# Expert turns with the two down pieces in third and fourth place, a TensorE sum of expert rows, and later stores of normed rows

## The reference, cut to what matters

```python
    def expert_block(args):
        xblk, e = args
        gate, up = jnp.split(xblk @ w13[e], 2, axis=-1)
        return (jax.nn.silu(gate) * up) @ w2[e]
    contrib = yb[dest] * sw[:, None].astype(h.dtype)
    return jax.ops.segment_sum(contrib, stok, num_segments=T)
    f = _hier_moe(u2, w_route_g, b_route_g, w_route_e, b_route_e, w_moe_13, w_moe_2)
    x = _layernorm(ALPHA * x + (1 + g2) * f, ln_ffn_g, ln_ffn_b)
```

## Time and profile before

| what | value |
|---|---|
| median of 3 runs | 2646.61 us (2645.77 to 2648.37) |
| the profiled execution | 2651.25 us, its span 2649.5 us |
| PE busy in the span | 2383.2 us (90%) |
| DVE, ACT, POOL busy | 1628.0, 1164.9, 543.3 us |
| mean granted TensorE clock | 0.956 |

### The profile page before, as it was taken

One profiled execution on the slowest core, in us unless ns is written; L12 is line 12 of the kernel. 1 busy time (PEld: TensorE's weight loads), 2 busy tenths in 40 slices (PEclk: granted clock), 3 DMA queues, 4 the chain that ended last, 5 costly groups with the idle time before them and its releaser, 6 DMA issues. The chain is left out here.

```text
span 2649.5 us, 32426 instructions
## 1 busy us (share of the span) xinstructions
PE 2383.2 (90%) x13016; PEld 1987.3 (75%) x13016; DVE 1628.0 (61%) x2532; ACT 1164.9 (44%) x1453; POOL 543.3 (21%) x309
## 2 busy tenths in 40 slices
PE   4999899999999999999999999999389999999960
PEld 2978888898888887667999978744267777777740
DVE  5269889889898870000333311176668888888869
ACT  2336766776766762000000000000167777777751
POOL 1211212212212120001443311000022332322320
PEclk8899999999999999999999999999599999999985
DMA  9272232233223215121111221211479999999953
GB/s 330 89 266 65 75 107 75 79 84 95 79 68 112 82 45 178 32 56 37 44 48 48 71 82 40 84 63 50 159 248 347 340 350 351 359 343 346 341 199 144
DMA packets 247177, 398.08 MB, mean 150 GB/s; under 512 B 17997, under 2 KB 168149, under 8 KB 243917
## 3 DMA queue, kind: packets, MB, share of 16 engines
q1 hardware_dynamic: 224050, 345.35, 39.3%
q0 software_dynamic: 14048, 34.39, 3.4%
q10 hardware_dynamic: 8928, 16.26, 1.9%
HBM read 365.23 MB, written 48.14 MB: 156 GB/s over the span
## 5 line engine op out<-in xcount | busy, mean ns | idle before, releaser
L2002 PE MATMUL bank<-u_hi,w_pairs 128*128 128x344 f32 x1344 | 450.4, 335 | 1.4 <-DVE u_lo L1353 1.4
L2004 PE MATMUL bank<-u_hi,w_pairs 128*128 128x344 f32 x1344 | 434.6, 323 | 0.0
L2003 PE MATMUL bank<-u_lo,w_pairs 128*128 128x344 f32 x1344 | 434.3, 323 | 0.0
L1737 DVE TENSOR_TENSOR we_parts<-u_whole,we_parts 128x2048 fp32r<-128x2048 f32 x129 | 295.1, 2288 | 57.9 <-ACT we_parts L1178 57.7
L1178 ACT ACTIVATE we_parts<-u_whole 128x2048 fp32r<-128x2048 f32 x129 | 247.1, 1917 | 51.4 <-PE bank L2283 26.5
L794 POOL TENSOR_TENSOR w_pairs<-arena,w_pairs 128x1024 fp32r<-128x1024 f32 x56 | 151.7, 2710 | 564.7 <-ACT w_pairs L954 564.5
L2002 PEld LDWEIGHTS bank<-u_hi,w_pairs 128*128 128x128 f32 x1344 | 257.7, 192 | 12.2 <-issue 10.5
L2003 PEld LDWEIGHTS bank<-u_lo,w_pairs 128*128 128x128 f32 x1344 | 257.3, 191 | 3.8 <-issue 3.8
L2004 PEld LDWEIGHTS bank<-u_hi,w_pairs 128*128 128x128 f32 x1344 | 257.1, 191 | 0.0
L2141 PE MATMUL bank<-arena 128*128 128x344 f32 x768 | 222.2, 452 | 0.0
L2281 PE MATMUL bank<-we_parts,x_parts 128*128 128x512 f32 x512 | 209.7, 410 | 3.3 <-DVE we_parts L1737 1.8
(11 more groups left out here) (345 smaller groups left out, 4956.2 us busy)
## 6 DMA issues: line engine op xcount, KB each, us to landing
u_whole<-in_w_moe_dram SPq DMA_DIRECT2D x128, 1024.0 KB, 7.4
arena<-in_w_moe_dram SPq DMA_DIRECT2D x64, 1024.0 KB, 7.4
arena<-in_w_in_dram SPq DMA_DIRECT2D x88, 512.0 KB, 5.4
arena<-in_w_ada_dram SPq DMA_DIRECT2D x24, 1024.0 KB, 7.1
arena<-cum_dram ACTq DMA_DIRECT2D x62, 256.0 KB, 3.2
yb_dram<-arena POOLq DMA_DIRECT2D x8, 1032.0 KB, 5.2
arena<-in_state_ssm_dram SPq DMA_DIRECT2D x16, 512.0 KB, 5.1
out_dram<-arena SPq DMA_DIRECT2D x16, 512.0 KB, 5.1
```

Source lines behind the costliest of these rows:

```text
L1737: dve.tensor_tensor(w_los[v], wraw[slot], w_his[v].bitcast(F32), ALU.subtract).then_inc(wlo_ready, 1)
L2002: pe.matmul(out, hi[:, k, :], u_hi[:, k, at], start=(k == 0), stop=False)
L2003: pe.matmul(out, hi[:, k, :], u_lo[:, k, at], start=False, stop=False)
L2004: last = pe.matmul(out, lo[:, k, :], u_hi[:, k, at], start=False, stop=(k == KD - 1))
```

## The change

Three parts. **Start:** the four head loads go behind the first weight unit and count on another semaphore, which TensorE awaits before its first dt product; VectorE's copy of `dskb` goes behind the last tile's low part; GpSimd awaits all eight products of the first conditioning third before its first store of normed rows. **Expert turns:** the order of pieces becomes gate 0, gate 1, down 0, down 1, gate 2, gate 3, on SP, ScalarE, VectorE and TensorE; h is turned after the whole of gate 0; ScalarE's output copies go behind the split of the sixth piece, VectorE's first subtraction ahead of the low part of h. In the drain there are two dummy slices. **End:** VectorE makes 18 diagonal matrices of routing weights once (`spread_f`, 128 x 2304); TensorE multiplies them with `fa` and `fb` and sums in the accumulator, four matmuls of 512 columns a tile, two tiles in flight; VectorE multiplies the sum by the gate in two halves. ScalarE's scaling and VectorE's L1908 go.

```diff
-                     (dtb, ...), (alog, ...), (dskb, ...), (w_dt, ...)]
+                     (rows_s[5:29, :], t["state_ssm_conv"][0].rearrange("b r d -> (b r) d"))]
+            heads = [(dtb, ...), (alog, ...), (dskb, ...), (w_dt, ...)]
...
-            for u in range(6):
+            load_unit(0, group_cols(0)[0])
+            for dst, src in heads:
+                sp.dma_start(dst, src).then_inc(finw_landed, 16)
+            for u in range(1, 6):
                 load_unit(u, group_cols(0)[u])
...
             pool.wait_ge(consts_ready, 1)
+            pool.wait_ge(mod_done, 8)
             for i in range(TILES + 1):
                 pool.wait_ge(x0_ready, i + 1)
...
-                        if j in (1, 2):
-                            load_w2(j - 1, before)
+                        if j in (2, 3):
+                            load_w2(j - 2, before)
                         else:
-                            load_w13(j, max(j - 2, 0), expert)
+                            load_w13(j, j if j < 2 else j - 2, expert)
...
             def expert_turn(b, n, stored):
                 silu(1 - b, n - 1)
                 w_high(n, 2)
                 h_high(1 - b, n - 1)
                 w_high(n, 3)
                 w_high(n, 4)
-                out_rows(1 - b, n - 1, n * 6 + 1, stored)
                 w_high(n, 5)
+                out_rows(1 - b, n - 1, n * 6 + 2, stored)
...
             w_high(extra * 2 + (2 * PAIRS), 2)
             h_high(1, extra * 2 + (2 * PAIRS - 1))
+            w_high(extra * 2 + (2 * PAIRS), 3, True)
...
-                act.wait_ge(fin_landed[i % 3], 32 * (i // 3 + 1))
-                act.activation(fa[i % 3][0:rows, :], fa[i % 3][0:rows, :], ACT.Copy,
-                               scale=wts[0:rows, i:i + 1]).then_inc(f_scaled, 1)
...
             def expert_turn(b, n, column, done_column):
                 h_both(1 - b, n - 1)
+                w_low(n, 2)
                 h_low(1 - b, n - 1)
-                for j in range(2, 6):
+                for j in range(3, 6):
                     w_low(n, j)
...
+            dve.tensor_tensor(spread_f, widen(ident, 1, 2 * NI), widen(wts, 2, P), ALU.mult).then_inc(spread_f_ready, 1)
...
-                fin.did(dve.scalar_tensor_tensor(x, fb[i % 3][0:rows, :], wts[0:rows, NI + i:NI + i + 1], x,
-                                                 ALU.mult, ALU.add))
-                fin.settle()
-                fin.did(dve.tensor_tensor(x, x, g2, ALU.mult))
+                dve.wait_ge(f_summed, i + 1)
+                for half in range(2):
+                    at = slice(512 * half, 512 * half + 512)
+                    last = dve.tensor_tensor(x[:, at], banks[2 * (i % 2) + half][0:rows, :], g2[:, at], ALU.mult)
...
-                    gate_up(b, n, 0, 0, (0,))
+                    gate_up(b, n, 0, 0).then_inc(wparts_used, 1)
                     turn_h(1 - b, n - 1)
-                    gate_up(b, n, 0, 0, (1,)).then_inc(wparts_used, 1)
+                    gate_up(b, n, 1, 1).then_inc(wparts_used, 1)
...
-                    down(1 - b, n - 1, 0, 2, n * 6).then_inc(wparts_used, 1)
-                    down(1 - b, n - 1, 1, 0, n * 6 + 1).then_inc(wparts_used, 1)
+                    down(1 - b, n - 1, 0, 0, n * 6 + 1).then_inc(wparts_used, 1)
+                    down(1 - b, n - 1, 1, 1, n * 6 + 2).then_inc(wparts_used, 1)
-                gate_up(b, n, 1, 1 + skip).then_inc(wparts_used, 1)
                 turn_rows(1 - b, n + 1, 0, landed)
...
+            for i in range(TILES + 1):
+                rows = P if i < TILES else NS
+                pe.wait_ge(fin_landed[i % 3], 32 * (i // 3 + 1))
+                if i >= 2:
+                    pe.wait_ge(f_scaled, i - 1)
+                for half in range(2):
+                    for a, rows_of in enumerate((fa, fb)):
+                        last = pe.matmul(banks[2 * (i % 2) + half][0:rows, :], spread_f[0:rows, a * NI + i, 0:rows],
+                                         rows_of[i % 3][0:rows, 512 * half:512 * half + 512],
+                                         start=(a == 0), stop=(a == 1))
+                last.then_inc(f_summed, 1)
```

More of the change, by code:

```diff
@@ L696, in load_w2 @@
             def load_w2(x, expert):
-                sp.dma_start(wraw[1 + x].rearrange("p (k c) -> p k c", k=2),
-                             w2_v[:, ds(expert * 4 + 2 * x, 2), :]).then_inc(wraw_landed[1 + x], 16)
+                sp.dma_start(wraw[2 + x].rearrange("p (k c) -> p k c", k=2),
+                             w2_v[:, ds(expert * 4 + 2 * x, 2), :]).then_inc(wraw_landed[2 + x], 16)
             sp.wait_ge(wo_done, TILES + 1)
             sp.wait_ge(u2_ready, TILES + 1)
-            for x, j in enumerate((0, 3, 4, 5)):
+            for x, j in enumerate((0, 1, 4, 5)):
                 load_w13(j, x, 0)
@@ L732, in _ @@
             expert = expert_of(extra * 2 + (2 * PAIRS - 1))
-            sp.wait_ge(wlo_ready, extra * 12 + (12 * PAIRS - 7))
-            sp.dma_start(wraw[0][:, 0:P], w13_v[:, 0, 0:P]).then_inc(wraw_landed[0], 16)
             for x in range(2):
-                sp.wait_ge(wlo_ready, extra * 12 + (12 * PAIRS - 6 + x))
+                sp.wait_ge(wlo_ready, extra * 12 + (12 * PAIRS - 7 + x))
+                sp.dma_start(wraw[x][:, 0:P], w13_v[:, 0, 0:P]).then_inc(wraw_landed[x], 16)
+            for x in range(2):
+                sp.wait_ge(wlo_ready, extra * 12 + (12 * PAIRS - 5 + x))
                 load_w2(x, expert)
@@ L1149, in _ @@
                 rows = P if i < TILES else NS
-                act.wait_ge(mvar_ready, i + 1)
+                act.wait_ge(var_ready, TILES + 2 + i)
                 act.activation(mv2[0:rows, i % 2, 2:3], mv2[0:rows, i % 2, 1:2], ACT.Sqrt,
-                               bias=epsc[0:rows, :]).then_inc(mstd_ready, 1)
+                               bias=epsc[0:rows, :]).then_inc(std_ready, 1)
                 act.wait_ge(u2_turned, i + 1)
@@ L1167, in _, with w_high @@
             act.activation(wb, wb, ACT.Exp).then_inc(route_e, 1)
-            def w_high(n, j):
+            def w_high(n, j, last=False):
                 g = slot_no(n, j)
                 first = isinstance(n, int) and n == 0
-                slot = (0, 3, 4, 5)[j] if first else j
-                act.wait_ge(wraw_landed[slot], n * 16 + (0 if slot in (1, 2) else 16))
-                if not (first and j < 3):
+                slot = (0, 1, 4, 5)[j] if first else j
+                act.wait_ge(wraw_landed[slot], n * 16 + (0 if slot in (2, 3) else 16))
+                if last:
+                    act.wait_ge(wlo_ready, g - 2)
+                elif not (first and j < 3):
                     act.wait_ge(wparts_used, g - 2)
@@ L1293, in _ @@
             last.then_inc(cols_copied, 1)
-            dve.wait_ge(small_landed, 16 * 16)
-            for h in range(2):
-                st.did(dve.tensor_copy(dskip[HD * h:HD * h + HD, :],
-                                       dskb[HD * h:HD * h + HD, :].rearrange("p (j h) -> p h j", h=2)[:, h, :]))
             for half in range(2):
@@ L1311, in _ @@
                 norm(i)
+            dve.wait_ge(small_landed, 12 * 16)
             add_mod(0)
@@ L1360, in _ @@
             u_low(TILES)
+            dve.wait_ge(finw_landed, 64)
+            for h in range(2):
+                st.did(dve.tensor_copy(dskip[HD * h:HD * h + HD, :],
+                                       dskb[HD * h:HD * h + HD, :].rearrange("p (j h) -> p h j", h=2)[:, h, :]))
             dve.wait_ge(x0_stored, 9 * 16)
@@ L1732, in w_low @@
             def w_low(n, j):
-                slot = (0, 3, 4, 5)[j] if isinstance(n, int) and n == 0 else j
+                slot = (0, 1, 4, 5)[j] if isinstance(n, int) and n == 0 else j
                 v = parts_of(n, j)
@@ L1905, in _ @@
                 x = fa[i % 3][0:rows, :]
-                dve.wait_ge(fin_landed[i % 3], 32 * (i // 3 + 1))
-                dve.wait_ge(f_scaled, i + 1)
-                fin.did(dve.scalar_tensor_tensor(x, fb[i % 3][0:rows, :], wts[0:rows, NI + i:NI + i + 1], x,
-                                                 ALU.mult, ALU.add))
-                fin.settle()
-                fin.did(dve.tensor_tensor(x, x, g2, ALU.mult))
-                fin.settle()
+                dve.wait_ge(f_summed, i + 1)
+                if i == 0:
+                    fin.settle()
+                for half in range(2):
+                    at = slice(512 * half, 512 * half + 512)
+                    last = dve.tensor_tensor(x[:, at], banks[2 * (i % 2) + half][0:rows, :], g2[:, at], ALU.mult)
+                    if half == 0:
+                        fin.did(last)
+                last.then_inc(f_scaled, 1)
+                dve.wait_ge(f_scaled, i + 1)
                 fin.did(dve.scalar_tensor_tensor(x, x1[0:rows, i, :], ALPHA, x, ALU.mult, ALU.add))
```

44 lines of the change are left out of this document (26 added, 18 removed).

## The result

The kernel after takes 2589.92 us (median of 4 runs, 2588.68 to 2590.84), the kernel before 2647.49 (median of 4, 2645.77 to 2648.71): a ratio of 0.978, 95% interval 0.9769 to 0.9792, or 57.6 us less. The forecast was 2590 us. That the total is met to a tenth of a us is partly luck: the start gave 2 to 3 us less than forecast and the expert turn some 4 us more, as the table of marks shows. The profiled execution after took 2590.1 us (span 2588.3).

A forecast was written before the change was run, and what follows sets the result against it. Prediction: start waits for data, the expert turn is a 19.61 us chain of waits without transfers, VectorE bounds the end. Terms -6.7 - 45 + 0.5 - 5.7 = -56.9 us, from median 2646.61 to 2590 us; range 2580 to 2622.

The forecast's parts named there:

- Start, -6.7: Start: conditioning piece 3, and the third's addition with it, comes 6.7 us earlier; ends -3 and -7.2.
- the heads at 2.9: Start: the four head loads, some 1400 pieces of 128 bytes, leaving the queue give 2.9 us; ends 1.0 and 3.4.
- Expert turn, -45: Expert stage: the turn falls from 19.70 to 18.2 us, 30 intervals x 1.5, -45 us.
- the closed chain: Expert turn: longest chain of waits, from output copy through splits, subtractions, h and 36 matmuls to the second output copy, 18.2 us.
- the forecast's two bounds: Expert stage, weight rate: 358 GB/s gives 19.1 us a turn, -18 us; 412 GB/s gives no limit, -45 us.
- Drain, +0.5: After the last turn: first down piece waits for a subtraction instead of h's high part, +0.5 us; ends 0 and +2.3.
- End, -5.7: End: VectorE tiles -11.5 us, TensorE's first sum +4.3, later sums +1.5; together -5.7 us, ends -9 and -2.7.
- ring: End: later sums sit in three buffers, 6.0 to 7.2 us a tile; 7.0 taken for six tiles, +1.5 us.
- Weights as the bound: Rival, expert stage: at 358 GB/s the turn is 19.1 us, total -29.9, 2617 us; 27%.
- A new wait in the old one's place: Rival, expert turn: stays at 19.7 us, only start, drain and end count, -11.9, 2635 us; 8%.
- The scatter: Slower rival, expert turn: output copies wait for scatter landing; at 18 us landing the turn is 20.9, 2671 us; 6%.
- The ends at nothing: Rival: sums stay at half clock, stores collide with weight units; both ends give nothing, the turn its 45, 2602 us; 6%.

The follow-up runs named there:

- The exchange on ScalarE: Fourth piece's split put ahead of the copy of h's high part: on the kernel after 2590.69 us; on the light kernel 2589.77 us.
- the light kernel: Kernel after with two of three gate and up products left out, 40 matmuls a turn instead of 72: 2595.37 us (one run).
- the run with the end alone: Kernel before with only the end changed (rows summed by TensorE, spread matrix, VectorE's new order): 2642.2 us, ratio 0.998.

## Why the prediction was right, term by term

*Start, -6.7.* Measured -3.7 to -4.8, inside the ends. The step that failed is "3 x 0.52 MB at the 412 GB/s that weight loads reach alone is 3.8 us", with its twin, the heads at 2.9. They measure 2.3 and 1.8 at piece 3. Both took a lone stream's rate for a queue in which other small pieces stay. The fixed distance from piece 3 to the addition (21.3 us) held: 21.15. The nine store issues were hidden as said (43.33 to 48.72 us on GpSimd, the projections start at 70.0); that the split behind them meets VectorE's scale step, before and after, the forecast did not see.

*Expert turn, -45.* Measured -48.2 with the drain. The stall went from 1.33 to 0, as forecast (0.1), and the turn to 18.07 instead of 18.2; 30 x 0.13 = 3.9 is the difference. Right was that TensorE's 72 matmuls and three transpositions are the next limit; the closed chain of about that length, on which 18.2 rested, is not what sets it, since TensorE waits for nothing in the stage. It has little to spare: h is done at 2424.70 us, and its transposition begins at 2424.81. (The exchange on ScalarE tries another chain, that of the light kernel.) The limit of the rate lies between the forecast's two bounds, 358 and 412 GB/s: it is 388. The value taken, no limit, was good by a margin of 3%, less than the forecast let see.

The Trainium skill ("DMA: Bandwidth & Descriptors", Bandwidth) has about 358 GB/s as one core's limit, and in the same section ties the figure to both cores of a pair streaming. This program runs on one core, and its rows show 378 and 388 GB/s, so 358 is no limit here. The Trainium skill ("HBM Reference", Specifications (TRN2)) has about 425 GB/s for a core that streams alone. The 388 lie below that.

*Drain, +0.5.* The last two output copies lie 21.83 us apart before and 20.19 after, that is 2.13 and 2.12 more than a turn: it cost nothing.

*End, -5.7.* Measured -6.1. First sum 5.73 (5.5 forecast; 6.79 in the run with the end alone), tile 6.74 to 6.81 (6.72), ring 0.6 instead of 1.5: only one of six tiles waited.

*The rivals.* Weights as the bound: not so at 378 GB/s, but so 3% further on. A new wait in the old one's place: not in this change; in the run with the transposition moved alone it is what happened. The scatter: landing, counted from the issue, fell from 9.8 to 7.9 us instead of growing, and ScalarE's copies wait for none; the fall is only a wait that now stands ahead of the issue (last section). The ends at nothing: both gave their part.

## What to carry to other kernels

A stall between two engines is worth what lies between it and the next wait on the same way: moving one instruction passed most of 1.33 us on to the next steps, and the whole reordering, with a piece of independent work in between, removed it. When a stall goes, lay out all limits of the loop beside each other; here TensorE (18.07), the chain to h (done 0.1 us before TensorE needs it) and the weights (17.6) lie within 0.5 us a turn, so a cut in one of them alone can give at most that. Price a transfer taken out of a mixed queue by what the queue then does, not by the rate of a lone stream.

## What the runs showed of the hardware that was not expected

GpSimd and VectorE stop each other. VectorE's 128x72 operation on two SBUF operands took 0.23 us with GpSimd not splitting and 1.18, 1.51, 2.04 and 2.31 us beside a GpSimd split, each time to the split's end; the run that holds the split back until the scale step is done, shows it by an edit. The reverse is read from rows alone and was not tried by itself: the scatters' issue on GpSimd took 2.89 us before, where it began within a subtraction of VectorE, and 1.01 after, where it began ahead of one. That makes up the scatter's shorter landing, but it is no gain: the wait has moved to the small 128x1 multiplication that GpSimd does ahead of the scatter, which takes 0.21 us before and 2.36 after, where it begins with a subtraction. From the start of that multiplication to the landing it is 10.2 us in the turn shown before and 10.4 after, with the median landings. Kernel before, timeline:

```profile
2472.33 0.21 POOL L881 TENSOR_TENSOR arena<-arena 128x1 f32<-128x1 f32 x1
2472.39 2.30 DVE L1737 TENSOR_TENSOR we_parts<-arena,we_parts 128x2048 fp32r<-128x2048 f32 x1 [0.39 <-ACT we_parts L1178]
2472.70 2.89 POOL L874 DMA_INDIRECT rows_dram<-arena  x1 [0.16 <-POOL arena L881]
```

Kernel after:

```profile
2473.49 2.36 POOL L888 TENSOR_TENSOR arena<-arena 128x1 f32<-128x1 f32 x1
2473.51 2.31 DVE L1745 TENSOR_TENSOR we_parts<-u_whole,we_parts 128x2048 fp32r<-128x2048 f32 x1 [1.11 <-ACT we_parts L1187]
...
2476.02 1.01 POOL L881 DMA_INDIRECT rows_dram<-arena  x1 [0.16 <-POOL arena L888]
...
2476.34 2.28 DVE L1745 TENSOR_TENSOR we_parts<-arena,we_parts 128x2048 fp32r<-128x2048 f32 x1
```

The Trainium skill ("SBUF — State Buffer", SBUF: two separate sides) has the two engines share one pair of ports as an exclusive lock, held for the whole instruction by whichever starts first, for a VectorE operation with two SBUF inputs among others (there against a GpSimd operation that reads SBUF). These rows agree, but for the order in the last case: by its record the multiplication begins 0.02 us ahead of the subtraction and still lasts to its end.

TensorE that is given less work can lose clock: at 74% busy with pauses of 1 to 2.4 us in each turn its granted clock was 0.83 in the mean, and the loop was no faster with 40 matmuls a turn (18.4 us) than with 72 (18.07). The other way round, 44 matmuls without use ahead of the first sum brought that sum from 5.73 us at a mean granted clock of 0.64 to 3.71 us at 1.00.
